# Three slabs instead of two summed tile by tile at the end of each output stage, and half of the next stage's transposes moved between its first products

## What is computed

```python
for layer in range(2):
    mix = mixer_ab(h, ...) if layer == 0 else mixer_c(h, ...)      # ends in y @ w_out
    h = layer_norm(DN_ALPHA * h + mix, ln_g[layer, 0], ln_b[layer, 0])
    ffn = peer(h, ...)                                             # ends in coef @ v
    h = layer_norm(DN_ALPHA * h + ffn, ln_g[layer, 1], ln_b[layer, 1])
# third block, with 16 meta tokens ahead of the 256:
h = h + hybrid_mixer(rmsnorm(h, g_mix), ...)                       # "s", ends in y @ w_out
h = h + peer_ffn(rmsnorm(h, g_ffn), ...)
out = rmsnorm(h, g_final)
```

## Time and profile before

| what | value |
|---|---|
| median of 3 runs | 2897.73 us (2896.16 to 2899.25) |
| the profiled execution | 2895.88 us, its span 2894.1 us |
| TensorE busy | 2864.6 us, 99% of the span |
| VectorE, ScalarE, GpSimd busy | 67%, 54%, 31% |
| HBM read | 509.20 MB, 177 GB/s over the span |

### The profile page before, as it was taken

One profiled execution on the slowest core, in us unless ns is written; L12 is line 12 of the kernel. 1 busy time (PEld: TensorE's weight loads), 2 busy tenths in 40 slices (PEclk: granted clock), 3 DMA queues, 4 the chain that ended last, 5 costly groups with the idle time before them and its releaser, 6 DMA issues.

```text
span 2894.1 us, 59555 instructions
## 1 busy us (share of the span) xinstructions
PE 2864.6 (99%) x21501; PEld 2616.7 (90%) x21501; DVE 1948.3 (67%) x3378; ACT 1550.7 (54%) x2516; POOL 894.3 (31%) x361
## 2 busy tenths in 40 slices
PE   8999999999999999999999999999999999999999
PEld 7899999888888889999998888889899999988887
DVE  4388577787557637947778855675539667788655
ACT  4444544677555544454467745654544544577554
POOL 3689600000004368970000000255779910000000
PEclk9999999999999999999999999999999999999999
DMA  6566655555765455565555576443566655555665
GB/s 215 169 181 186 183 170 171 172 177 175 240 191 167 146 169 181 182 187 169 173 170 176 178 235 195 149 135 121 165 192 188 182 176 171 170 176 176 208 192 164
DMA packets 146464, 515.21 MB, mean 178 GB/s; under 512 B 17552, under 2 KB 18576, under 8 KB 146336
## 3 DMA queue, kind: packets, MB, share of 16 engines
q1 hardware_dynamic: 146336, 513.46, 57.0%
HBM read 509.20 MB, written 4.19 MB: 177 GB/s over the span
## 4 chain that ended last, share of the span: by engine, by line
PE 92%; DVE 2%; POOL 2%; ACT 1%; issue 1%; DMA 0%; SPq 0%; DVEq 0%; ACTq 0%; POOLq 0%
PE col L601 15%; PE col L603 15%; PE col L602 15%; PE acc L601 13%; PE acc L603 13%; PE acc L602 13%; POOL w_lo L552 2%; PE col L797 2%; PE acc L797 2%; PE acc L755 1%; ACT w_hi L915 1%; DVE acc L1224 0%; PE acc L2420 0%; PE acc L736 0%; PE misc L2433 0%
## 5 line engine op out<-in xcount | busy, mean ns | idle before, releaser
L552 POOL TENSOR_TENSOR w_lo<-ring,w_hi 128x1024 fp32r<-128x1024 f32 x357 | 894.1, 2516 | 1433.6 <-ACT w_hi L915 1432.7
L915 ACT ACTIVATE w_hi<-ring 128x1024 fp32r<-128x1024 f32 x941 | 993.8, 1056 | 540.2 <-PE acc L603 441.5
L601 PE MATMUL col<-x_hi,w_hi 128*128 128x256 f32 (+2 forms) x3896 | 1102.4, 283 | 1.7 <-POOL w_lo L552 1.3
L602 PE MATMUL col<-x_lo,w_hi 128*128 128x256 f32 (+2 forms) x3896 | 1096.3, 281 | 0.0
L603 PE MATMUL col<-x_hi,w_lo 128*128 128x256 f32 (+2 forms) x3896 | 1095.8, 281 | 0.0
L552 DVE TENSOR_TENSOR w_lo<-ring,w_hi 128x1024 fp32r<-128x1024 f32 x584 | 713.9, 1223 | 368.8 <-ACT w_hi L915 365.3
L601 PEld LDWEIGHTS col<-x_hi,w_hi 128*128 128x128 f32 x3896 | 735.5, 189 | 5.1 <-issue 3.2
L603 PEld LDWEIGHTS col<-x_hi,w_lo 128*128 128x128 f32 x3896 | 736.6, 189 | 0.0
L602 PEld LDWEIGHTS col<-x_lo,w_hi 128*128 128x128 f32 x3896 | 732.5, 188 | 0.7
L601 PE MATMUL acc<-w_hi,c_hi 128*128 128x512 f32 x1664 | 653.5, 393 | 1.0 <-issue 1.0
L603 PE MATMUL acc<-w_hi,c_lo 128*128 128x512 f32 x1664 | 648.2, 390 | 0.0
(11 more groups left out here) (317 smaller groups left out, 1952.5 us busy)
## 6 DMA issues: line engine op xcount, KB each, us to landing
ring<-in_u SPq DMA_DIRECT2D x384, 512.0 KB, 3.6
ring<-in_v SPq DMA_DIRECT2D x384, 512.0 KB, 4.0
ring<-in_wq SPq DMA_DIRECT2D x48, 512.0 KB, 3.8
ring<-in_s_in SPq DMA_DIRECT2D x21, 512.0 KB, 3.4
ring<-in_c_in SPq DMA_DIRECT2D x16, 512.0 KB, 3.7
ring<-in_s_out SPq DMA_DIRECT2D x16, 512.0 KB, 3.3
ring<-in_s_gate SPq DMA_DIRECT2D x12, 512.0 KB, 3.3
ring<-in_s_conv SPq DMA_DIRECT2D x12, 512.0 KB, 3.2
```

The source lines that it names most:

```text
L552: eng.tensor_tensor(k.w_lo[s.slot][:, :], k.ring[s.slot][:, :], k.w_hi[s.slot][:, :].bitcast(F32), ALU.subtract).then_inc(k.lo[s.slot], 1)
L601: pe.matmul(out, a[0], b[0], start=start, stop=False, **kw)
L602: pe.matmul(out, a[0], b[1], start=False, stop=False, **kw)
L915: act.activation(k.w_hi[s.slot][:, :], k.ring[s.slot][:, :], ACT.Copy).then_inc(k.hi[s.slot], 1)
```

## The change

Seven edits in one:

1. The tail of an output stage (not of ab) takes three slabs tile by tile. Banks 0 and 1 of all three come first, with bank 2 of the first of them ahead of the last slab; then bank 2 of the other two (`tile_full`), then bank 3 of all three.
2. The residual of all banks stands behind the fourth last slab (before, that of banks 2 and 3 stood behind the third last).
3. In the layers half-major (peer0, c, peer1) only the first two transposes of halves stand ahead of the first products, elsewhere in a paired stage the first three. The others stand behind the first eight products of the first slab.
4. Stage s begins with a pair as well.
5. The order of the norm on VectorE: `scale` of the first half right behind `inverse`, ahead of the statistics of the last bank, and in half-major stages `centre` and `scale` of tile 1's first half ahead of the second half of tile 0.
6. ScalarE rounds the first slab of the next stage behind the first deviation (or behind the third of the four squares) where it stood ahead of them; the other orders around it follow.
7. Fewer matmuls of `keep_busy`.

```diff
-BUSY = {..., "peer2": (12, 6, 6)}
+BUSY = {..., "peer2": (8, 6, 3)}
-PAIRED = ("peer0", "c", "peer1", "peer2")
+PAIRED = ("peer0", "c", "peer1", "s", "peer2")
-def added_behind(back, late):
-    if late:
-        return (0, 1, 2) if back == 3 else ()
-    return {4: (0, 1), 3: (2,)}.get(back, ())
+def tiles_first(name):
+    return 2 if half_major(name) else 3
...
     def fresh_pair(self, s, name, cols=T):
...
+        w.next(k.xhi, tiles_first(name))
+        with_hi(s, 0)
+        self.transpose_left()
+        self.bank_free(second)
+        self.slab_ready(second)
+        with_hi(second, 0)
+        w.next(k.xhi, BANKS - tiles_first(name))
+        with_hi(s, 1)
+        with_hi(second, 1)
         w.next(k.x_ready, 2)
+        with_lo(s, 0)
+        w.next(k.x_ready, 2)
+        with_lo(s, 1).then_inc(k.used, 1)
+        with_lo(second, 0)
+        with_lo(second, 1).then_inc(k.used, 1)
...
     def while_normed(self, before_s):
...
-            self.keep_busy(12)
+            self.keep_busy(10)
...
-                    self.keep_busy(8 if n == 1 else 0)
+                self.keep_busy(6 if n == 1 else 0)
...
+    def row_tail(self, end, begin):
+        k, pe, w = self.k, self.pe, self.w
+        slabs = range(end - SLOTS, end)
+        for n in range(begin, end - SLOTS):
+            self.row_slab(Slab(n), marks=(0, 1, 2) if n == end - SLOTS - 1 else ())
+        def part(n, bank):
+            ...
+            if n == slabs[0]:
+                w.next(k.resid)
+            return self.split_matmuls(...)
+        for n in slabs:
+            if n == slabs[-1]:
+                part(slabs[0], 2)
+            pe.wait_ge(k.coef[n % SLOTS], k.rows_in_slot(Slab(n), 1))
+            self.slab_ready(Slab(n))
+            part(n, 0)
+            ins = part(n, 1)
+        ins.then_inc(k.tile_full, 1)
+        part(slabs[1], 2)
+        part(slabs[2], 2).then_inc(k.tile_full, 1)
+        for n in slabs:
+            part(n, 3).then_inc(k.used, 1)
...
-                dve.wait_ge(k.used, last - 1)
+                dve.wait_ge(k.used, last + 1 - behind)
...
         w.next(k.param[slot], 32)
         centre(0, 0)
+        stats(1, 0)
         ready = inverse(0)
+        scale(0, 0, ready)
         stats(1, 1)
         moments(1)
-        scale(0, 0, ready)
         if first:
             centre(1, 0)
-            ready = centre(0, 1)
             ready = inverse(1)
             scale(1, 0, ready)
+            ready = centre(0, 1)
             done = centre(1, 1)
             scale(0, 1, ready)
             scale(1, 1, done)
```

More of the change, by code:

```diff
@@ L628, in features, with fresh_pair, with_hi, with_lo @@
         ins.then_inc(k.used, 1)
-    def fresh_pair(self, s, name):
+    def fresh_pair(self, s, name, cols=T):
         k, pe, w = self.k, self.pe, self.w
[L633 to L644, removed]
-        w.next(k.x_ready, 2)
[L646 to L651, removed]
+        halves = (range(0, DC // 2), range(DC // 2, DC))
+        def with_hi(s, half):
+            hi, lo = slab_view(k, s)
+            for c in halves[half]:
+                pe.matmul(k.col[s.slot][:, 0:cols], hi[:, c, :], k.x_hi[:, c, 0:cols], start=c == 0, stop=False)
+                pe.matmul(k.col[s.slot][:, 0:cols], lo[:, c, :], k.x_hi[:, c, 0:cols], start=False, stop=False)
+        def with_lo(s, half):
+            hi, _ = slab_view(k, s)
+            for c in halves[half]:
+                ins = pe.matmul(k.col[s.slot][:, 0:cols], hi[:, c, :], k.x_lo[:, c, 0:cols], start=False,
+                                stop=c == DC - 1)
+            return ins
+        second = s + 1
+        self.bank_free(s)
+        self.slab_ready(s)
+        w.next(k.xhi, tiles_first(name))
[7 more added lines that the diff above has]
+        with_hi(second, 1)
+        w.next(k.x_ready, 2)
+        with_lo(s, 0)
[3 more added lines that the diff above has]
+        with_lo(second, 1).then_inc(k.used, 1)
@@ L678, in wide, with rows @@
         ins.then_inc(k.used, 1)
-    def rows(self, s, y_hi, y_lo, start, stop, marks=(), holds=()):
+    def rows(self, s, y_hi, y_lo, start, stop, marks=()):
         k = self.k
@@ L873, in row_stage @@
         if to is None:
-            self.row_tail(first + count, first + begin, late)
+            (self.row_tail_late if late else self.row_tail)(first + count, first + begin)
 def tensor_program(k, pe):
@@ L984, in tile_squares, with summed_square @@
         self.tile_std(t)
[L986 removed]
+    def summed_square(self, t, half, last):
         k = self.k
[L989 to L995 removed]
+        if half == 0:
+            self.w.next(k.tile_full)
+        elif t:
+            self.act.wait_ge(k.used, last + 1)
+        self.square(k.acc[t * 2 + half][:, :], 2 * t + half)
     def finish(self, name, end):
@@ L1181, in rest_x, with residual @@
         w.skip(k.xhi, 4)
-    def residual(self, banks, last, alpha):
+    def residual(self, banks, last, alpha, behind=3):
         k, dve = self.k, self.dve
@@ L1295, in finish_rms @@
         self.mean_square(1, 1)
[L1296 to L1297 removed]
+        self.rms_norm(1, slot, summed=True, between=lambda: keep(1, 1))
     def mean_square(self, t, squares=2):
@@ L1318, in rms_norm @@
             cut = slice(half * 512, (half + 1) * 512)
+            if half and between is not None:
+                between()
             if not summed:
@@ L1812, in vector @@
             e.coef(self.y[:, n, :], Slab(out + n))
-        e.residual(range(BANKS), out + 7, DN_ALPHA)
+        e.residual(range(BANKS), out + 7, DN_ALPHA, behind=2)
 class MixC:
```

91 lines of the change are left out of this document (48 added, 43 removed).

## The result

The changed kernel took a median of **2903.68 us** over 21 runs (2900.06 to 2906.71); the kernel before 2897.41 us over 21 runs (2895.5 to 2899.8). The ratio is 1.002, with a 95% interval of 1.0014 to 1.0026: 6.3 us slower, where 0.8 us of gain was forecast and 2899.6 was the upper end of the range. The profiled execution took 2903.34 us, its span 2901.5, 7.4 more than before.

A forecast was written before the change was run, and what follows sets the result against it. TensorE, busy 99% of the span, was taken as the bound, with only six hand-overs to win from. Their terms, 0.36 + 0.27 + 0.59 - 0.72 + 0.41 - 0.07, gave 0.84 us gained: 2896.9 us, range 2893.9 to 2899.6.

The forecast's parts named there:

- ScalarE's new order: At the hand-overs, the next stage's first w_hi waits for a late slot; costed at nothing, slack 1.5 us.
- the clock: Rival: granted clock falls at hand-overs, 1.4 us each; one or two falling 0.10 (2898.3 to 2899.7), all five 0.03.
- the rival in which all five hand-overs fall: Granted clock falls at every one of five hand-overs, 1.4 us each, giving 2903.9 us; chance 0.03.
- The fewer unused matmuls: At hand-overs, six for eight end just as the second transpose may start; costed at nothing.
- The sentence on transposes: Skill page quoted for the clock rival: a transpose does not count as busy time the way a product does.
- peer1 to s: Hand-over into stage s: no gain from an earlier full tile, later centres and four transposes cost time; together -0.72 us.
- the new order of the norm: At peer1 to s, centre waits for moments that statistics covered before; 0.22 us added as a loss.
- four transposes: Transposes moved behind the first products take TensorE's time; 0.5 us per set of four.
- TensorE never waited from 1858.21 on: In the old stage s TensorE had no waits, so pairing slabs there wins nothing.
- The tail's waits: Output-stage tails: TensorE stalls 0.77 us in peers for bank 2's residual, 0.45 in c and s for GpSimd's w_lo.
- The three half-major hand-overs: ab to peer0 +0.36, peer0 to c +0.27, c to peer1 +0.59 us, all gains.
- s to peer2: Hand-over from s: first product 0.68 us earlier, 0.23 from the tail, less 0.5 for four transposes; +0.41 us.

The follow-up runs named there:

- first set: Follow-up kernels made from the changed kernel with one thing altered each; its own runs of the kernel before had a median of 2897.45 us.
- the covered version: Changed kernel plus one-tensor-input addition, third slab of s rounded behind the last x_hi, and unused matmuls in the hand-over waits: 2898.00 us, ratio 1.0.
- the second experiment: Changed kernel, but ScalarE rounds the third slab of s behind its last x_hi, not behind the second deviation: 2901.88 us, ratio 1.0011.
- the fourth experiment: Changed kernel, but stage s begun as before the change, one slab first and all sixteen transposes ahead: 2900.41 us, ratio 1.0012.

## Why the prediction was wrong

- **The step that failed is "ScalarE's new order", "Costed at nothing; slack 1.5".** The slack was reckoned against TensorE, which needs `w_lo`; and there it holds. What I didn't ask is what else GpSimd's later work meets. It moved under VectorE's operations with two SBUF inputs. In the changed kernel that is two holds of 1.9 and 1.1 (2.05 and 1.27 less 0.15), 3.0 us. Taking 2.2 of it away (one tensor input) moved the median by 3.4, a size at the limit of what two medians can tell. Edit 6 alone costs 4.2, with the clock in it; and the tail alone has the hold as well, since its slots come free late.
- **The second is the clock, a rival at 0.10 and 0.03.** It was priced at 1.4 a place; by the traces it cost 2.5 at the hand-over and some 1.5 inside s (at most 1.7). Its likelihood was far too low. That 2903.9, the rival in which all five hand-overs fall, lies next to the measured time is luck: one hand-over fell, and one place inside s. The argument against it was "that the waits grow by well under a us, and that products start sooner". But edits 3 and 4 take transposes away from ahead of the first product and put a wait of 0.78 there, and with no wait above 0.94 in the hand-over they lost 3.7. Covering gave 3.1 back, at the edge of what can be told, and gave the kernel before nothing. The mean granted clock of the runs agrees: of 21 runs of the changed kernel 12 stood at 0.997 and 8 at 0.998, one at 0.999; of 33 runs of before (first set) one stood at 0.997, 16 at 0.998 and 16 higher; of 11 of the covered version eight stood at 0.999 and one at 1.0. At 2900 us a thousandth is 2.9 us. The fewer unused matmuls, "Costed at nothing", were that for edit 7 alone (ratio 1.0002), but not in the change, since edits 3 and 4 asked for more of them. The sentence on transposes that I quoted from the Trainium skill, page "TensorE: Matmul & The Clock Gate", Part 4: PE-mode transpose, can't be judged from these runs: in none of them did only the kind of TensorE's work change.
- **peer1 to s, -0.72, measured -5.25.** Without hold and clock it is -0.83: from the first statistics to the first product the second experiment, which has no hold here, takes 13.56 (1845.07 to 1858.63) where before took 13.15 (1845.06 to 1858.21), so the new order of the norm costs 0.41 and not the 0.22 added; four transposes cost 0.42 and not 0.5. On top come the hold, 1.9, and the clock, 2.5, which makes 5.2.
- **"TensorE never waited from 1858.21 on"** isn't so: it waits 2.44 at 1897.15. Pairing slabs doesn't shorten that wait (2.49), so the conclusion that the pair wins nothing was right. That it was worse than nothing is a hint only (2.8 less without it, in the fourth experiment).
- **The tail's waits, 0.77 and 0.45**: right in place and releaser. The idle times are 0.63 in the three peers, 0.33 in c, 0.28 in s; the delay is 0.93 at the last row product of peer0, and 0.62 in c (1041.38 for 1040.72, the rows ahead of the wait being 0.04 apart), so more than reckoned in both.
- **The three half-major hand-overs, 1.22 and not 0.18.** The first product came at +7.84 and not +7.53, most of it because tile 1's scale came 0.22 later than reckoned. The stretch from it to the third slab grew by 0.91 where 1.0 was reckoned (the eight transposes took 0.80). So the new order gave 0.14 in each, not 0.36. The rest of the shortfall stands ahead of the first statistics: they came 0.24 later at peer0 to c where 0.09 was reckoned, 0.1 later at ab to peer0 where nothing was, and at c to peer1 0.08 earlier where 0.23 was reckoned.
- **s to peer2, +0.41**: measured -0.75; the hold there (1.1) is the difference. With the addition on one tensor input the first product came 7.62 behind the first square (2082.80 to 2090.42), where 7.65 was forecast.

By the profiles the 7.5 us of the table are the two holds, 3.0, the clock at two places, 4.0, and 0.4 to 0.5 for all the rest, which the forecast had as a gain of 0.84. By the medians only the whole can be told: 5.8 came back with the holds gone and the waits covered. Why the clock falls at these places in one execution and not in another stays open.

## What to carry to other kernels

When an edit delays work on an engine that has slack, list what runs on the other engines at its new time, not only who waits for its result: here GpSimd's 128 x 1024 operations held VectorE's operations with two SBUF tensors as inputs, of 128 x 1 and of 128 x 512 elements, until the running instruction ended (2.05 for 0.15 us, 2.10 for 1.42). A scalar operand in place of the second tensor avoided it (0.20). An idle time in a profile is not what a wait costs: 0.63 of idle time put the last row product off by 0.93. And where transposes or other TensorE work is moved out of a hand-over, put unused matmuls into the waits that it leaves: the full clock behind one hand-over was worth 2.5 us here, more than the 0.84 that the whole change was to win.

## What was not expected of the hardware

- The hold ends with the GpSimd instruction that is running, in all seven profiles that show it to within 0.05 us (three of them: 1854.99 against 1854.98, 1857.46 against 1857.45, 2091.75 against 2091.7), and hits 128 x 1 elements (2.05 for 0.15). Before the change the addition missed it by 0.1 us.
- With the third slab late, the clock fell in the hand-over behind waits of 0.89, 0.82 and more (0.61 from 1857 to 1860, with 2.05 of 3.00 us busy). In the kernel before it stood at 1.00 behind a wait of 2.44. Behind that same wait inside s the profiles of ten kernels show a fall (0.5 to 0.7 in the lowest window of 3 us) and those of six none, with kernels of one slab and of the pair on both sides; where the wait was covered, neither of two shows one. The length of a wait alone doesn't decide it; what does stays open.
